# Second block of a two-block transformer kernel: value projections placed between the first attention steps, values read three steps late, first tile's norm interleaved with the second's

## The reference, cut to what matters

```python
sh1, sc1, g1, sh2, sc2, g2, sh3, sc3, g3 = jnp.split(mod, N_MOD, axis=-1)
h = rmsnorm_2(x, norm_pre[l, 0]) * (1.0 + sc1) + sh1
y = swiglu(h, ffn_w_gate[l, 0], ffn_w_up[l, 0], ffn_w_down[l, 0])
x = x + 0.5 * g1 * rmsnorm_2(y, norm_post[l, 0])
h = rmsnorm_2(x, norm_pre[l, 1]) * (1.0 + sc2) + sh2
y = hybrid_mixer(h, mix_w_in[l], mix_b_in[l], mix_w_out[l], attn_sinks[l], group_gain[l], rel_bias)
x = x + g2 * rmsnorm_2(y, norm_post[l, 1])
h = rmsnorm_2(x, norm_pre[l, 2]) * (1.0 + sc3) + sh3
y = swiglu(h, ffn_w_gate[l, 1], ffn_w_up[l, 1], ffn_w_down[l, 1])
x = x + 0.5 * g3 * rmsnorm_2(y, norm_post[l, 2])
```

## Time and profile before

| | |
|---|---|
| median of 3 runs | 4192.07 us (4189.42 to 4196.15) |
| profiled execution | 4185.77 us |
| span of its records | 4184.0 us |
| second block, from its first transposes (L2657) | 2875.3 to the end |
| PE busy over the span | 83% |
| DVE, POOL, ACT busy | 58%, 27%, 16% |
| mean granted TensorE clock | 0.916 |

### The profile page before, as it was taken

How to read it: one execution, slowest core, us unless ns; L and a number is a source line. 1 busy time by engine, 2 the same in 40 slices (tenths; PEclk the granted TensorE clock), 3 DMA queues, 4 the chain that set the end, 5 groups by cost and what they waited for, 6 DMA issues and landing times. The chain is left out here.

```text
span 4184.0 us, 41280 instructions
## 1 busy us (share of the span) xinstructions
PE 3481.7 (83%) x14658; PEld 2595.5 (62%) x14658; DVE 2434.6 (58%) x4688; ACT 656.1 (16%) x1790; POOL 1130.6 (27%) x1032
## 2 busy tenths in 40 slices
PE   8999986898888999988976552325998999998899
PEld 4678874787777777766862221114766676777576
DVE  2654778887778676757559998874443101442301
ACT  2521112600000000025021110001011201001300
POOL 0000000165665555510037777772000000000000
PEclk8999997999999999999997876657998999998999
DMA  4566554899999999962869999997863244783143
GB/s 169 161 179 195 140 176 171 263 409 409 408 408 366 409 409 408 409 234 57 246 227 367 407 374 382 407 380 273 304 216 121 91 161 151 261 285 121 61 161 111
DMA packets 560603, 1096.72 MB, mean 262 GB/s; under 512 B 29940, under 2 KB 343284, under 8 KB 559126
## 3 DMA queue, kind: packets, MB, share of 16 engines
q1 hardware_dynamic: 408824, 554.12, 39.1%
q0 software_dynamic: 147456, 536.94, 32.9%
q10 hardware_dynamic: 4128, 3.15, 0.3%
HBM read 1078.36 MB, written 15.73 MB: 261 GB/s over the span
## 5 line engine op out<-in xcount | busy, mean ns | idle before, releaser
L2039 PE MATMUL ps<-gv,diag 128*128 128x512 f32 x512 | 295.8, 743 | 388.6 <-DMA gv<-in_v_tab,eid 245.9
L2513 PE MATMUL ps<-hT,wring 128*128 128x256 f32 x2560 | 561.6, 380 | 2.8 <-DMA wring<-in_ffn_w_up 2.8
L1671 PE MATMUL ps<-hT,wring 128*128 128x256 f32 x2048 | 484.4, 391 | 83.9 <-DVE hT L1843 81.2
L1705 POOL DMA_INDIRECT gu<-in_u_tab,eid x256 | 287.5, 1123 | 976.9 <-POOLq L133 622.0
L2513 PEld LDWEIGHTS ps<-hT,wring 128*128 128x128 f32 x2560 | 487.4, 191 | 86.8 <-issue 12.4
L1671 PEld LDWEIGHTS ps<-hT,wring 128*128 128x128 f32 x2048 | 388.0, 194 | 175.8 <-DVE hT L1843 123.0
L2039 PEld LDWEIGHTS ps<-gv,diag 128*128 128x128 f32 x512 | 120.9, 244 | 561.5 <-issue 406.3
L1662 PE MATMUL ps<-hT,wring 128*128 128x256 f32 x2048 | 464.4, 380 | 1.0 <-ACT G L1743 1.0
L1662 PEld LDWEIGHTS ps<-hT,wring 128*128 128x128 f32 x2048 | 390.6, 191 | 53.9 <-issue 1.1
L1867 DVE SCALAR_TENSOR_TENSOR wring<-gv,wgt,wring 128x1024 f32<-128x1024 f32 x254 | 326.6, 1286 | 106.1 <-DMA gv<-in_v_tab,eid 99.8
L1850 DVE CUSTOM_DVE_ANT_0 gu<-gu,htok 128x1024 f32<-128x1024 f32 x256 | 313.2, 1223 | 126.8 <-DMA gu<-in_u_tab,eid 124.5
(11 more groups left out here) (382 smaller groups left out, 4313.4 us busy)
## 6 DMA issues: line engine op xcount, KB each, us to landing
wring<-in_u_first SPq DMA_DIRECT2D x128, 512.0 KB, 9.0
wring<-in_v_tab SPq DMA_DIRECT2D x128, 512.0 KB, 6.8
room<-in_ada_w SPq DMA_DIRECT2D x32, 1536.0 KB, 11.4
wring<-in_ffn_w_gate SPq DMA_DIRECT2D x44, 1024.0 KB, 9.2
wring<-in_ffn_w_up SPq DMA_DIRECT2D x44, 1024.0 KB, 11.7
wring<-in_ffn_w_down SPq DMA_DIRECT2D x44, 1024.0 KB, 5.0
wring<-in_w_in SPq DMA_DIRECT2D x72, 512.0 KB, 6.7
wring<-in_w_mod SPq DMA_DIRECT2D x28, 1024.0 KB, 5.6
```

The source lines that it names most:

```text
L1671: m = nc.tensor.matmul(ps[:, n // 2, (n % 2) * S:(n % 2 + 1) * S], vslot[:, e % 2, n * P:(n + 1) * P], act_[:, e % 3, :], start=e == 0 and ...
L1705: nc.gpsimd.indirect_dma_start(gu[:, n % RING, :], None, ub, bass.IndirectOffsetOnAxis(ap=eid[:, n // COLS, n % COLS:n % COLS + 1], axis=0 ...
L2039: m = nc.tensor.matmul(ps[:, mixed_banks(t) + b, :], diag[:, s, i, :], gv[:, d + i, b * 512:(b + 1) * 512], start=first, stop=last)
L2513: m = mm(ps[:, b + n, q * S:(q + 1) * S], up_slot(s, q)[:, k, n * P:(n + 1) * P], hT[:, k, 0:S], start=k == 0, stop=k == KD - 1)
```

## The change

- **Value weights.** The ring slots of the mixer's five loads become (1, 0, 1, 1, 0), and the shared keys (u = 3, 512 KB) get a place of their own in slot 1 behind the others (columns 4096 on) and a semaphore of their own. So u = 4 is issued when tile 8 of 13 is done, u = 3 already when the last-but-one `down_` is.
- **Value projections.** They leave `projection` and are four calls `project_v(l, g)`: group 0 ahead of `scores(0)`, groups 1 to 3 in steps 0 to 2 of the attention loop. VectorE takes them in (`place_v`) ahead of its part of steps 0 to 3.
- **Order in a step.** TensorE: scores(i), turn(i-2), values(i-3) (was i-1 and i-2), 19 steps in place of 18. ScalarE: copy(i-2) before the two Exp (was copy(i-1) after them).
- **Columns.** All 24 (was 8) stand in one run behind feed-forward 2l, the late shifts and scales are made in `enter(3l+1)` by `late_mod`; steps 1 to 4 lose their 16.
- **Gate rows of X = 3l+2** leave the end of feed-forward 2l+1: TensorE makes them right after attention, before `turn_h`; VectorE's four operations stand at the start of the feed-forward; the gate's load goes to SP's queue behind `mix_w_out`.
- **Group norm of tile 0.** Collect after step 11 (was 10), squares and root after step 12 (was 11), normalize 13 (was 12), place after the loop (was step 14); turn_y in step 15 (was 13), project from step 16 (was 14).
- **Leave and enter.** ScalarE starts the squares of the new x's first tile before the root of the second tile's y, VectorE makes the last quarter of x after the first tile's sum; the ScalarE half of h of tile 0 stands before the root of tile 1.

```diff
         def mix_slot(l, u):
-            return (u + 1 + FLIP[2 * l]) % 2
+            return ((1, 0, 1, 1, 0)[u] + FLIP[2 * l]) % 2
         def proj_slot(l, u):
-            return self.wring[:, mix_slot(l, u), 0:KD * W[u]].rearrange("p (k n) -> p k n", k=KD)
+            first = 4096 if u == 3 else 0
+            return self.wring[:, mix_slot(l, u), first:first + KD * W[u]].rearrange("p (k n) -> p k n", k=KD)
...
-                    for u in range(5):
-                        if u < 2:
-                            sp.wait_ge(gu.sem, 2 * NCH * (2 * l + 1) - 2 * (1 - u))
-                        else:
-                            sp.wait_ge(full.sem, 17 * l + last_of[u - 2])
-                        if u == 4:
-                            sp.wait_ge(yfull.sem, 4 * (3 * l + 1))
-                        sp.dma_start(proj_slot(l, u), w_all[:, :, at[u]:at[u] + W[u]]).then_inc(wm[mix_slot(l, u)].sem, 16)
+                    for u in range(2):
+                        sp.wait_ge(gu.sem, 2 * NCH * (2 * l + 1) - 2 * (1 - u))
+                        load(u, wm[mix_slot(l, u)])
+                    sp.wait_ge(down.sem, (NCH - 1) * (2 * l + 1))
+                    load(3, wmk)
+                    sp.wait_ge(full.sem, 17 * l + last_of[0])
+                    load(2, wm[mix_slot(l, 2)])
+                    sp.wait_ge(full.sem, 17 * l + last_of[1])
+                    sp.wait_ge(yfull.sem, 4 * (3 * l + 1))
+                    load(4, wm[mix_slot(l, 4)])
...
+                def project_v(l, g):
+                    t, c = divmod(g, 2)
+                    if g == 0:
+                        pe.wait_ge(wm[mix_slot(l, 4)].sem, 16 * nth_mix(l, 4))
+                    pe.wait_ge(outd.sem, 17 * l + (7, 8, NFM + 1, NFM + 2)[g])
+                    for k in range(KD):
+                        m = mm(ps[:, 2 + c, 0:VW // 2], hT[:, k, t * P:(t + 1) * P],
+                               proj_slot(l, 4)[:, k, c * (VW // 2):(c + 1) * (VW // 2)], start=k == 0, stop=k == KD - 1)
+                    m.then_inc(full.sem, 1)
...
-                    pe.wait_ge(outd.sem, 17 * (l + 1))
-                    for i in range(2 * NP + 2):
+                    project_v(l, 0)
+                    pe.wait_ge(outd.sem, 17 * l + NFM)
+                    for i in range(2 * NP + 3):
                         if i < 2 * NP:
                             scores(i)
-                        if 1 <= i <= 2 * NP:
-                            turn(i - 1)
-                        if i == NP + 2:
+                        if 2 <= i <= 2 * NP + 1:
+                            turn(i - 2)
+                        if i < 3:
+                            project_v(l, i + 1)
+                        if i == 3:
+                            pe.wait_ge(outd.sem, 17 * l + NFM + 2)
+                        if i == NP + 3:
                             pe.wait_ge(coefd.sem, 3 * l + 2)
-                        if i >= 2:
-                            values(i - 2)
-                        if 1 <= i <= 4:
-                            columns(2, 20 + 4 * i, 24 + 4 * i, 24, i == 4)
+                        if i >= 3:
+                            values(i - 3)
                         if i == 5:
+                            pe.wait_ge(outd.sem, 17 * (l + 1))
                             gate_row(3, 3 * l + 1, 0)
                         if i == 6:
-                            pe.wait_ge(modd.sem, l + 1)
                             gate_row(2, 3 * l + 1, 1)
-                        if i == 13:
+                        if i == 2 * NP - 1:
                             turn_y(0)
-                        if i >= 14:
-                            project(0, 2 * (i - 14), 2 * (i - 13))
-                    project(0, 8, 16)
+                        if i >= 2 * NP:
+                            project(0, 2 * (i - 2 * NP), 2 * (i - 2 * NP) + 2)
+                    project(0, 6, 16)
...
                 for l in range(2):
                     feed_forward(2 * l)
-                    columns(4, 8, 16, 8, True)
+                    columns()
                     turn_h(3 * l + 1)
                     projection(l)
                     attention(l)
+                    for c in range(2):
+                        gate_row(6 + c, 3 * l + 2, c)
                     turn_h(3 * l + 2)
...
                 def enter(E):
-                    for t in range(2):
-                        square_x(E, 2 * t)
-                        square_x(E, 2 * t + 1)
-                        root_x(E, t)
-                    for t in range(2):
-                        act.wait_ge(inv2.sem, 2 * E + t + 1)
-                        run(yc[:, t, 512:D], x2[:, t, 512:D], ACT.Copy, scale=stat[:, E, 12 + t:13 + t]).then_inc(hb.sem, 1)
+                    square_x(E, 0)
+                    if E:
+                        root_y(E - 1, 1)
+                    square_x(E, 1)
+                    root_x(E, 0)
+                    square_x(E, 2)
+                    square_x(E, 3)
+                    half_h(E, 0)
+                    root_x(E, 1)
+                    half_h(E, 1)
...
                     for i in range(2 * NP):
                         t, j = divmod(i, NP)
                         nk = P * (t + 1)
+                        if i >= 2:
+                            copy(i - 2)
                         act.wait_ge(mready.sem, 16 * l + i + 1)
-                        if i >= 2:
-                            act.wait_ge(tfull.sem, 16 * l + i - 1)
...
-                        if i >= 1:
-                            copy(i - 1)
-                        if i == 11:
-                            group_sums(0)
+                        if i == 12:
+                            group_squares(0)
+                            group_root(0)
...
                 def enter(E):
...
+                    sum_x(E, 0)
+                    if E:
+                        new_x(E - 1, 3)
+                    half_h(E, 0)
+                    sum_x(E, 1)
+                    half_h(E, 1)
+                    if E % 3 == 1:
+                        late_mod(E // 3)
```

More of the change, by code:

```diff
@@ L2507, in gate_up @@
                         return
+                    if j == 1 and F % 2:
+                        pe.wait_ge(coefd.sem, 3 * (F // 2) + 3)
                     for n in range(2):
@@ L2533, in gate_row, with columns @@
                     mm(ps[:, b, :], ones[:], lsum[:, n:n + 512], start=True, stop=True).then_inc(rowfull.sem, 1)
-                def columns(b, first, last, at0, ends):
-                    for n in range(first, last):
-                        m = mm(ps[:, b, 2 * (n - at0):2 * (n - at0) + 2], lsum[:, n * P:(n + 1) * P], ones[:, 0:2], start=True, stop=True)
-                    if ends:
-                        m.then_inc(colfull.sem, 1)
+                def columns():
+                    for i, n in enumerate((*range(8, 16), *range(24, 40))):
+                        m = mm(ps[:, 4, 2 * i:2 * i + 2], lsum[:, n * P:(n + 1) * P], ones[:, 0:2], start=True, stop=True)
+                    m.then_inc(colfull.sem, 1)
                 def feed_forward(F):
@@ L2687, in square_x @@
                     act.wait_ge(xd.sem, 4 * E + i + 1)
+                    if i < 2 and E:
+                        act.wait_ge(ysq.sem, 4 * (E - 1) + i + 3)
                     if i >= 2:
@@ L2774, in _ @@
                         enter(3)
+                root_y(5, 1)
             @block.vector
@@ L2989, in _ @@
                         enter(3)
+                new_x(5, 3)
     def build(self):
```

125 lines of the change are left out of this document (67 added, 58 removed).

## The result

The changed kernel took 4124.19 us (median of 4 runs, 4120.64 to 4140.88) beside 4193.8 (4189.42 to 4196.15) for the kernel before: a ratio of 0.984, with a 95% interval of 0.982 to 0.987. It is 68 to 70 us faster; 4136 was forecast. The profiled execution took 4120.64 us with a span of 4118.9, 65.1 less than before, at a mean granted clock of 0.926 (0.916 before).

The account below looks back on a forecast made before the run. TensorE was taken to bound the second block, losing time to waits and half clock. Gains of 49 (stretches), 3.5 (gate rows), −0.8 (columns) and 3.9 (leave and enter) sum to 55.6 us: 4136 us, range 4117 to 4160.

Parts of the forecast that it names:

- rival C: Attention: group norm finds cover in two steps of distance, clock doesn't fall after it; 4121 us, chance 0.15.
- The stretches: Mixer, tile 13's end to last product of project: 86.8 us a layer, a gain of 24.5 each, 49 for two.
- Work at full clock: TensorE work in a layer's mixer stretch at the full 2.4 GHz, columns in the loop left out: 74.3 us.
- Waits: TensorE's waits in a layer's mixer stretch sum to 7.0 us, in place of 17.4.
- Half clock: A layer's mixer stretch: 1.0 us left in early steps, 4.5 behind the long wait; 5.5 in all.
- The wait before values(11): Attention: TensorE waits 3.0 us for a copy queued behind ScalarE's 4.3 us of group norm; old 3.22 us wait moved.
- rival B: Attention steps 3 to 8: half clock stays in thin work, 6.5 us more a layer; 4149 us, chance 0.22.
- Gate rows: Two matmuls a layer leave feed-forward 2l+1 for a wait for h: gain 1.7 to 1.88 per layer, 3.5 us.
- Columns: Entries 1 and 4: 34 records fit at full clock, the last 14 are slow; 0.8 us lost in all.
- Leave and enter: Sub-layer passages: h ready sooner, transposes end 0.9 us sooner at entry 3, 1.5 at 2 and 5; 3.9 in all.
- A: Attention: only the weight wait goes, loop bound by the chain VectorE, ScalarE, PE; gain 20, 4172 us, chance 0.08.
- D: Columns plus sparse passage to h drop the clock, half through projection and values; 4302 us if to step 15, chance 0.02.

Follow-up runs that it names:

- c3: Changed kernel with tile 0's group 1/root made by a shift, a subtraction and three Newton steps on VectorE instead of ScalarE's root; 4122.16 us.
- b1: Kernel before with only the weight loads in the changed order; 4181.39 us.
- b2: Kernel before with the weight loads in the changed order and all 24 columns in one run behind feed-forward 2l; 4161.12 us.
- a3: Changed kernel with the four value groups projected and taken in ahead of the attention loop again; 4135.2 us.
- a4: Changed kernel with turn(i-1), values(i-2) and copy behind the Exp again, value groups still between the scores; 4142.41 us.
- c2: Changed kernel with the gate rows of X = 3l+2 back at the end of feed-forward 2l+1; 4128.6 us.
- c1: Changed kernel with ScalarE's and VectorE's order in leave and enter as before the change; 4136.37 us.
- first repeat: Changed kernel run again, unaltered, in the second comparison; 4134.77 us.

## Why the prediction was right, and where its terms were off

The mechanism held: less waiting and less half clock in attention brought most of it. Forecast were 55.6 us; behind the first feed-forward the profiled execution shows 64.6. The measured 4124 is inside the range, 12 below the likeliest time and between the forecast's own spread (down to 4128) and rival C (4121).

**The stretches** were to be 86.8 us and are 82.36 and 84.12, so 7.1 of the 9 us that were missed. Of the sum's three terms the clock missed most. PE was busy 77.57 and 79.18 us, of which 3.41 and 6.67 at half clock. *Work at full clock*: 74.3 were forecast, 75.9 and 75.8 measured (77.57 − 1.7 and 79.18 − 3.3); c3, with the clock at 1.00 throughout, has 76.40. A value group is 4.30 us, as the forecast said; where the other 1.6 us lie was not taken apart. *Waits*: 7.0 were forecast and 4.79 and 4.94 measured. Three terms were near: 0.9 in step 10 (0.92), 3.0 before values(11) (2.76), 1.1 for place(1) (1.11). The 0.5 for turn(13) and the 1.4 of "handoffs too small to list" aren't there as idle time, but the work is longer by about as much: work and waits together were 81.3 in the forecast and are 80.7 and 80.8. *Half clock*: 5.5 were forecast, 1.7 and 3.3 measured; the 1.0 in the early steps didn't come, and the 4.5 behind the long wait was 2.8 and 1.2 too much. The same count gives 13.9 and 12.6 us for the kernel before, where the forecast had 16.3.

**The wait before values(11)** was right in size and partly by luck. The forecast had 4.3 us of group norm ahead of the copy, with the table back for Exp among them; by its own times the squares would then start 37.5 us into the stretch (42.4 − 4.3 − 0.6 for the copy). In the trace the copy has only 2.84 us of it ahead (3214.05 to 3216.89), the second load stands behind the copy, and the squares start at 39.8, after the 2.02 us that ScalarE waits for VectorE's collecting. The two errors nearly cancel: the copy ends at 43.2, forecast was 42.4, and PE itself gets there at 40.5 and not 39.4.

**The reason for the half clock** held. I named the waits of the first scores as what began it and the columns as what it lay over. In b1 it begins behind these waits, before the loop's first column, and with the columns lasts 17.1 us; in b2, without columns, it doesn't begin in layer 0 and lasts 3.4 us in layer 1. For my expectation of a3 I held thin steps with short waits to be enough for a long fall (rival B by another name), and a3 shows that they aren't.

**The share of each part**, which the sum had lumped together, is best read over both layers, since within one kernel a layer's stretch differs by 1.8 us with the length of the half clock. The stretches lost 56.0 us: 13.5 by the early weights (b1), 18.0 by the columns out of the loop (b2), and 24.5 by the new order in the loop from b2 to the changed kernel. Of that, a4 gives 10.7 to the step of distance with the copy's place, and a3 4.8 to the place of the value groups. The remaining 9, by subtraction, are the later group norm and turn_y of tile 0, or what the parts bring only together; neither was run alone.

**Gate rows**: 3.5 forecast; the four matmuls are 3.4, and c2 has 3.0 more in the two feed-forwards. **Columns**: 34 records were to fit at full clock, 3.7 us from the first, with 14 slow ones behind. The shape was right and the place of the fall wasn't: it came 4.21 us behind the first, so 39 records begin ahead of it and 9 take 0.21 each (44 and 3 in layer 1). The passage at entry 1 is 9.70 against 9.71, at entry 4 0.55 shorter. I had a loss of 0.8; it is a gain of 0.5, and chance decides between them. In the eight profiled executions with this order of columns the fall comes 2.2 to 5.6 us behind the first column, the run of 24 takes 5.42 to 8.18 us, and the passage is 3.05 to 3.35 us longer than the run every time: the transposes wait for the columns, and the passage is 8.5 to 11.5 us by where the clock falls.

**Leave and enter**: 3.9 forecast, 3.7 at entries 2, 3 and 5, 3.8 by c1. The reason that I gave for 1.5 at entries 2 and 5 against 0.9 at 3 fell: the gate rows were to keep PE working. In c2, without them, passages 2 and 5 are 7.88 as well. It is the interleaving that does it at all three (c1).

**The table switch.** The load is 1.28 us and the root starts 1.30 us after the load began; behind the second load the Exp starts 1.30 us after it as well. The Trainium skill (ScalarE: Activation LUTs, What ACT_TABLE_LOAD costs) counts a drain of about 1380 ns beside the load; this case's trace doesn't show it, before or after. In the new order only one load is ahead of the copy, so by that figure the wait of 2.76 us would be one drain longer, not two as the forecast had it.

**The clock and the busy share.** 76% busy at 1.00 in b2's layer 0 and 90% at 0.64 in b1 are the same steps, and PE's work in them differs by the 2-column matmuls alone. The Trainium skill (TensorE: Matmul & The Clock Gate, What's actually happening) says that activity releases the throttle; these rows don't refute it, but they show that the busy share of the profile can't be read as that activity.

**The rivals.** A (only the weight wait goes) would have been 4172: b1, which has the weight wait alone, is 4181, and the old distance put back (a4) costs 10.7 us in the stretches, so distance isn't moved waiting. B fell: steps 3 to 8 run at 1.00 (rows to 3203.53). D's long half clock didn't come. C's wait and clock came only with c3, and there as 4.2 us for both layers, not 15.

What stays open: why the half clock behind the wait of 2.76 us lasts 3.4 us in one layer and 6.8 in the other, which is nearly all that parts stretches of 82.4 and 84.1 us (the two change places in the first repeat); what decides where in the run of columns the clock falls; and the 9 us of the new order that no experiment took apart.

## What to carry to other kernels

Read the granted clock beside the busy share of each stretch: a stretch that is 90% busy at 0.64 has a third of its time to give. Here taking out the narrow matmuls gave it back (b2), and the half clock behind the longest wait went when that wait was cut in two (c3). Where latency rather than work sets a loop's pace, try a step more between the stages: here it was worth 10.7 us in the stretches, and filler between them 4.8. And keep the clock as a term of its own in a sum laid out by rows, with its count (time at half clock, times the busy share, halved) made for the kernel before: here work and waits came out within 0.7 us a layer, and the clock was 2 to 4 us off.

## What the runs showed of the hardware that I had not expected

- The clock fell within or just behind runs of 2-column fp32 matmuls although PE was busy all the time: behind a feed-forward at full clock, it was 1.00 for 4.21 us of the columns and 0.50 from there, with PE 100% busy in both (rows 3118.83 and 3123.04). A record takes 0.11 us at full and 0.21 at half. The same 48 records took 6.39 us there, 5.42 where the clock fell only behind them (c3, layer 1), and longer in others (a3, layer 1, in PE's timeline):

```profile
3747.91 7.88 PE L2546 MATMUL ps<-ones,lsum 128*128 128x2 f32 x48
```

- PE kept 1.00 through 24% of idle time with one gap of 1.72 us (b2, layer 0), and a gap of 1.65 us in the same steps of layer 1 was followed by 3.4 us at half. Behind the gap of 2.76 us the clock was at half for 3.4 or 6.8 us in every profiled execution that has it.
- The changed kernel reached the end of its first feed-forward in the second block at 3119, 3132 and 3171 us in three comparisons, and took 999.9, 999.6 and 997.4 us from there. Differences of 5 us can be read only from the part that an edit touches.
